# Seven instead of six of the eight contraction slices of the experts' gate and up products in upper and lower parts

## The reference, cut to what matters

```python
def moe(h, combine, w_gate, w_up, w_down):      # 16 experts, D_EXPERT = 256
    out = jnp.zeros_like(h)
    for e in range(N_EXPERTS):
        a = jax.nn.silu(h @ w_gate[e]) * (h @ w_up[e])
        out = out + combine[..., e:e + 1].astype(h.dtype) * (a @ w_down[e])
    return out
```

## Time and profile before

| | |
|---|---|
| median of three runs | 479.05 us (478.69 to 479.23) |
| the profiled execution | 479.01 us |
| its span in the trace | 477.3 us |
| TensorE busy | 431.7 us, 90% |
| VectorE busy | 313.1 us, 66% |
| ScalarE busy | 215.8 us, 45% |
| mean granted TensorE clock | 0.966 of full speed |

### The profile page before, as it was taken

The page is one execution under the profiler, slowest core; times in us unless marked ns, Lnnn a source line. Parts: engine busy times, 40 slices in busy tenths (PEclk is TensorE's granted clock), DMA queues, the critical chain, the costliest instruction groups (busy, mean ns, idle before and its releaser), DMA issues.

```text
span 477.3 us, 5118 instructions
## 1 busy us (share of the span) xinstructions
PE 431.7 (90%) x1824; PEld 280.4 (59%) x1824; DVE 313.1 (66%) x485; ACT 215.8 (45%) x360; POOL 107.4 (22%) x129
## 2 busy tenths in 40 slices
PE   5999999999999999999999999999999999998000
PEld 2444674477664544446687776777777777775000
DVE  3699969485403576776484166788778777783287
ACT  3121470151966810114211146788678777783151
POOL 7870000370065200000007410222332223211000
PEclk9999999999999999999999999999999999999655
DMA  8992007505993511110720249999999999611463
GB/s 271 381 359 81 0 2 109 126 22 153 409 420 137 214 56 44 44 44 12 297 90 0 36 145 426 408 421 419 406 373 368 377 396 356 247 52 43 150 251 149
DMA packets 37319, 98.95 MB, mean 207 GB/s; under 512 B 16976, under 2 KB 22688, under 8 KB 30624
## 3 DMA queue, kind: packets, MB, share of 16 engines
q1 hardware_dynamic: 28512, 88.45, 49.6%
q0 software_dynamic: 5088, 8.49, 5.0%
q10 hardware_dynamic: 3696, 1.71, 1.4%
HBM read 91.18 MB, written 14.17 MB: 221 GB/s over the span
## 4 chain that ended last, share of the span: by engine, by line
PE 73%; DVE 14%; DMA 5%; ACT 4%; issue 2%; SPq 1%; POOLq 0%; DVEq 0%; ACTq 0%
PE bank L1017 11%; PE bank L1189 9%; PE bank L858 6%; PE bank L1163 5%; PE bank L1168 4%; PE bank L1172 4%; PE bank L1176 4%; PE bank L1090 3%; PE bank L1092 3%; PE bank L1091 3%; DMA region_b<-in_ssm_par 3%; PE bank L1104 3%; PE bank L1147 3%; ACT region_a L632 2%; PE bank L874 2%
## 5 line engine op out<-in xcount | busy, mean ns | idle before, releaser
L1017 PE MATMUL bank<-region_b,region_e 128*128 128x512 f32 x128 | 58.3, 601 | 0.6 <-DVE region_f L1480 0.6
L858 PE MATMUL bank<-region_e,region_a 128*128 128x512 f32 x128 | 56.0, 595 | 0.0
L858 PEld LDWEIGHTS bank<-region_e,region_a 128*128 128x128 f32 x128 | 24.0, 190 | 29.7 <-issue 28.7
L1017 PEld LDWEIGHTS bank<-region_b,region_e 128*128 128x128 f32 x128 | 23.2, 190 | 25.0 <-issue 23.6
L1168 PE MATMUL bank<-gate_up_upper,tokens_upper 128*128 128x512 f32 x96 | 36.2, 459 | 0.0
L1172 PE MATMUL bank<-gate_up_upper,tokens_lower 128*128 128x512 f32 x96 | 29.8, 392 | 0.0
L1631 DVE TENSOR_TENSOR gate_up_lower<-region_a,gate_up_upper 128x1024 fp32r<-128x1024 f32 x24 | 28.0, 1221 | 2.4 <-ACT gate_up_upper L781 2.4
L517 POOL DMA_INDIRECT slot_scratch<-io_t,slot_i x8 | 8.5, 1058 | 93.4 <-issue 93.4
L530 POOL DMA_INDIRECT expert_scratch<-region_g,inv_t x8 | 11.4, 1429 | 78.4 <-ACT region_g L806 78.4
L865 PE MATMUL bank<-region_e,region_a 128*128 128x512 f32 x48 | 22.3, 627 | 5.0 <-DMA region_a<-in_w_in 5.0
L1090 PE MATMUL bank<-ple_gate_upper,hidden_upper 128*128 128x512 f32 x64 | 26.5, 415 | 0.0
(11 more groups left out here) (310 smaller groups left out, 936.4 us busy)
## 6 DMA issues: line engine op xcount, KB each, us to landing
region_a<-in_w_exp_gate SPq DMA_DIRECT2D x8, 1024.0 KB, 9.0
region_a<-in_w_exp_up SPq DMA_DIRECT2D x8, 1024.0 KB, 17.5
region_a<-in_w_exp_down SPq DMA_DIRECT2D x8, 1024.0 KB, 17.6
region_a<-in_w_in SPq DMA_DIRECT2D x3, 1536.0 KB, 17.8
region_b<-in_w_out SPq DMA_DIRECT2D x1, 4096.0 KB, 14.4
region_b<-in_w_exp_gate SPq DMA_DIRECT2D x4, 1024.0 KB, 9.5
region_b<-in_w_exp_up SPq DMA_DIRECT2D x4, 1024.0 KB, 17.5
region_b<-in_w_exp_down SPq DMA_DIRECT2D x4, 1024.0 KB, 17.3
```

Source lines behind the costliest of these rows:

```text
L858: last = mm(bank[bank_i][:], w[:, k, m * P:(m + 1) * P], xT[:, k, :], start=(k == 0), stop=(k == KD - 1))
L1017: last = mm(bank[WO_AT[half][group]][:], hdT[:, k, t * P:(t + 1) * P], w_o[:, k, half * 512:half * 512 + 512], start=(i == 0), stop=(i == ...
```

## The change

Seven slices go in parts, and one (slice 0) stays float32. The pieces in which the weights are rounded and subtracted are no longer three of two slices but four: `K_PARTS` has one slice first, and then three pieces of two. ScalarE's copy of the tokens is one slice in float32 and three and four slices rounded (before: two, two and four), VectorE's subtraction of the tokens three and four slices (before: two and four).

```diff
--- before.py
+++ after.py
@@ -41,7 +41,9 @@
 EPS = 1e-5
 NEG = -1.0e30
 BIG = 3.0e38
-KS = 6
+KS = 7
+K_PARTS = ((0, 1), (1, 3), (3, 5), (5, KS))
+NK = len(K_PARTS)
 CAP = P
 OVER = 7
 SLOT_TILES = NE + OVER
@@ -769,17 +771,17 @@
             def hgT_copy(e, r):
 
                 ac.wait_ge(S["pe_hgT"], e + 1)
-                a.activation(hgT[:, r, 0:2, :], bank[B_TOK[0]][:, 0:2 * P].rearrange("p (k s) -> p k s", k=2), ACT.Copy)
-                a.activation(x_hi[r][:, 0:2 * P], bank[B_TOK[0]][:, 2 * P:4 * P], ACT.Copy).then_inc(S["hgT_evac"], 1)
-                a.activation(x_hi[r][:, 2 * P:6 * P], bank[B_TOK[1]][:], ACT.Copy).then_inc(S["hgT_evac"], 1)
+                a.activation(hgT[:, r, 0, :], bank[B_TOK[0]][:, 0:P], ACT.Copy)
+                a.activation(x_hi[r][:, 0:3 * P], bank[B_TOK[0]][:, P:4 * P], ACT.Copy).then_inc(S["hgT_evac"], 1)
+                a.activation(x_hi[r][:, 3 * P:7 * P], bank[B_TOK[1]][:], ACT.Copy).then_inc(S["hgT_evac"], 1)
 
             def gate_up_upper(b, loads):
 
                 ac.wait_ge(S[f"e_in{b}"], 48 * loads)
-                for c in range(KS // 2):
-                    at = (KD - KS + 2 * c) * DE
-                    a.activation(gu_hi[:].rearrange("p (u n) -> p u n", u=2)[:, :, 2 * c * DE:2 * (c + 1) * DE],
-                                 ebuf[b][:, 0:4096].rearrange("p (u n) -> p u n", u=2)[:, :, at:at + 2 * DE], ACT.Copy).then_inc(S["gu_hi_set"], 1)
+                for lo, hi in K_PARTS:
+                    at = KD - KS
+                    a.activation(gu_hi[:].rearrange("p (u n) -> p u n", u=2)[:, :, lo * DE:hi * DE],
+                                 ebuf[b][:, 0:4096].rearrange("p (u n) -> p u n", u=2)[:, :, (at + lo) * DE:(at + hi) * DE], ACT.Copy).then_inc(S["gu_hi_set"], 1)
 
             def expert(e, b, loads, last=False):
                 r = b % 2
@@ -1161,18 +1163,18 @@
                 w_lo = gu_lo[b][:].rearrange("p (u k n) -> p k u n", u=2, k=KD)
                 for k in range(KD - KS):
                     mm(out_, hgT[:, r, k, :], w[:, k], start=(k == 0), stop=False)
-                C = KS // 2
-                for c in range(C):
+                C = NK
+                for c, ks in enumerate(K_PARTS):
                     pe.wait_ge(S["gu_hi_set"], C * e + c + 1)
-                    for k in (2 * c, 2 * c + 1):
+                    for k in range(*ks):
                         mm(out_, x_hi[r][:, k * P:(k + 1) * P], w_hi[:, k], start=False, stop=False)
                     if c == 0:
                         pe.wait_ge(S["gu_lo_set"], (C + 1) * e + 1)
-                    for k in (2 * c, 2 * c + 1):
+                    for k in range(*ks):
                         mm(out_, x_lo[:, k * P:(k + 1) * P], w_hi[:, k], start=False, stop=False)
-                for c in range(C):
+                for c, ks in enumerate(K_PARTS):
                     pe.wait_ge(S["gu_lo_set"], (C + 1) * e + c + 2)
-                    for k in (2 * c, 2 * c + 1):
+                    for k in range(*ks):
                         last = mm(out_, x_hi[r][:, k * P:(k + 1) * P], w_lo[:, KD - KS + k], start=False, stop=(k == KS - 1))
                 return last
 
@@ -1620,15 +1622,16 @@
 
                 dv.wait_ge(S["hgT_evac"], 2 * e + 2)
                 r = b % 2
-                tt(x_lo[:, 0:2 * P], bank[B_TOK[0]][:, 2 * P:4 * P], x_hi[r][:, 0:2 * P], ALU.subtract)
-                tt(x_lo[:, 2 * P:6 * P], bank[B_TOK[1]][:], x_hi[r][:, 2 * P:6 * P], ALU.subtract).then_inc(S["gu_lo_set"], 1)
+                tt(x_lo[:, 0:3 * P], bank[B_TOK[0]][:, P:4 * P], x_hi[r][:, 0:3 * P], ALU.subtract)
+                tt(x_lo[:, 3 * P:7 * P], bank[B_TOK[1]][:], x_hi[r][:, 3 * P:7 * P], ALU.subtract).then_inc(S["gu_lo_set"], 1)
                 w = ebuf[b][:, 0:4096].rearrange("p (u n) -> p u n", u=2)
                 w_lo = gu_lo[b][:].rearrange("p (u n) -> p u n", u=2)
                 w_hi = gu_hi[:].rearrange("p (u n) -> p u n", u=2)
-                for c in range(KS // 2):
-                    dv.wait_ge(S["gu_hi_set"], KS // 2 * e + c + 1)
-                    at = (KD - KS + 2 * c) * DE
-                    tt(w_lo[:, :, at:at + 2 * DE], w[:, :, at:at + 2 * DE], w_hi[:, :, 2 * c * DE:2 * (c + 1) * DE], ALU.subtract).then_inc(S["gu_lo_set"], 1)
+                for c, (lo, hi) in enumerate(K_PARTS):
+                    dv.wait_ge(S["gu_hi_set"], NK * e + c + 1)
+                    at = KD - KS
+                    tt(w_lo[:, :, (at + lo) * DE:(at + hi) * DE], w[:, :, (at + lo) * DE:(at + hi) * DE],
+                       w_hi[:, :, lo * DE:hi * DE], ALU.subtract).then_inc(S["gu_lo_set"], 1)
 
             def lower_parts(e, b):
```

## The result

The changed kernel takes 480.05 us (479.56 to 481.13, eight runs) where the kernel before takes 478.78 (478.43 to 479.27, eight runs). The ratio is 1.0025, its 95% interval 1.0015 to 1.0034: 0.7 to 1.6 us slower. The forecast was +0.8 us and 479.8 us.

What follows compares the result with a forecast made beforehand. Late landings of the down weights' loads were taken to stop TensorE's row; the longer chain behind them moved the last down products' start from 433.43 to 434.24, +0.81 us on 479.01, so 479.8 us, range 477.5 to 480.6.

Steps and rivals of the forecast that it cites:

- The bound: Experts' stage: landings of the down weights' loads, 10.0 us apart, stop TensorE's row of 9.71 us an expert.
- the window at 412 us: 412.0 to 417.1 us: DMA engines busy 0.47 on average, read as one or a few engines setting the landing.
- D(11): Start of the down matmuls behind expert 11's token transposes on TensorE; forecast within 0.1 us of before.
- A(13): ScalarE's start on expert 13's weights after waiting for their landing; 407.16 before, forecast within 0.3 us of it.
- The chain behind T: From an expert's token transposes through VectorE's subtractions to the next expert's down matmuls: 9.60 us before, 10.33 forecast.
- "0.56": VectorE: time between its last gate and up weights' piece and the down weights' subtraction, carried over unchanged in the sum.
- The chain behind A: From ScalarE's start on landed weights to the next expert's down matmuls: 7.49 us before, 8.00 forecast.
- hidden: ScalarE's fourth rounding piece, 0.51 us in a row, claimed to end before VectorE is ready for the down weights.
- A + 5.6: End of ScalarE's rounding of the down weights, counted in us from its start on the landed weights.
- The landings: Loads of the down weights: assumed to land unmoved; this case gave +0.81 us and had a chance of 0.55.
- load 13: Load of expert 13's down weights; every 0.1 us it lands late was priced as 0.1 us at the end.
- the fourth rival: Loads come later: requests slide with the down products, 0.3 to 0.9 us more, 480.4 with 0.6; chance 0.15.

Runs made afterwards that it cites:

- kernels without gathers: Kernel before and changed kernel, gathers of the tokens of experts 4 to 15 replaced by one 4 KB row each: 478.16 us (0.9983) and 476.54 us (0.9953).
- spread slots: Token slot s put on partition 2 (s mod 64) + s div 64: changed kernel 476.06 us (0.9943), kernel before 477.78 us (0.9969).
- products only: Kernel before with TensorE's part of the change alone, one float32 slice and seven in parts, suppliers as before: 479.16 us, ratio 1.0001.
- ScalarE cut: Parts only with ScalarE's small weights' piece cut from 2 x 256 to 2 x 16 columns, VectorE's left whole; run once for the trace, no time given.
- parts only: Changed kernel with its ScalarE and VectorE work kept, but TensorE doing two float32 slices and six in parts: 479.75 us, ratio 1.0019.
- its two cuts: Parts only with VectorE's, or else ScalarE's, small weights' piece cut from 2 x 256 to 2 x 16 columns; each run once for the trace, no time given.
- late wait: Changed kernel with the eight down matmuls needing only upper weights first, the wait for the lower part behind them: 479.81 us, ratio 1.0017.

## Why the prediction was right, and where it was not

**The number.** Forecast 479.8 us, measured 480.05; forecast +0.8 us, measured +1.27 by the medians. A part of the closeness is luck: the forecast was added to the profiled execution of before, 479.01 us, and the median of its eight runs is 478.78. The difference was 0.5 us short, mostly by the landings below.

**TensorE.** 0.17 us an expert was right: the full row is 9.53 us, forecast 9.55.

**The bound.** Right, and shown three times: TensorE's part alone gains nothing, the kernels without gathers gain 1.7 us, and so do those with spread slots. The reading of the window at 412 us, most DMA engines done and a few setting the landing, fits the runs with spread slots, though no view shows one engine. The Trainium skill (DMA: Bandwidth & Descriptors, "Why a DMA increments its semaphore by 16 and not by 1") says that the count is full only when the last engine has finished. That alone doesn't say that an earlier request lands no earlier, as the prediction had it; it takes a last engine that is never out of work as well. The runs bear the conclusion out where the slots are not spread: in products only D(11) is 0.46 us earlier than before and A(13) 0.10 later.

**The chain behind T.** Forecast 10.33 us, measured 7.69 + 2.29 + 0.14 = 10.12. The step that failed is "0.56" between VectorE's last piece and the down weights, which was carried over as if it were work. It was in part a wait for ScalarE (0.34 us is enough, as the rows with ScalarE cut show), whose rounding ends at 331.33 + 1.94 = 333.27 in the earlier trace rows and lets VectorE start at 333.30 in the earlier trace rows. The small piece came out as forecast: 4.09 us for four pieces against 3.50 for three, so 0.59 (forecast 0.60). Alone, behind a landing, it takes 0.69. The Trainium skill (VectorE: DVE Perf Modes, section on the TRN2 errata) has (N + 151) / 0.96 ns for it, 0.69 us, and the trace agrees. VectorE's four pieces in a row, and its rows at the landing of expert 13:

```profile
327.96 4.09 DVE L1633 TENSOR_TENSOR gate_up_lower<-region_b,gate_up_upper 128x512 fp32r<-128x512 f32 x4
...
407.24 0.69 DVE L1633 TENSOR_TENSOR gate_up_lower<-region_b,gate_up_upper 128x512 fp32r<-128x512 f32 x1 [0.53 <-ACT gate_up_upper L783]
...
411.60 0.42 DVE L1639 TENSOR_TENSOR act_lower<-bank,act_upper 128x256 fp32r<-128x256 f32 x1
412.16 2.29 DVE L1641 TENSOR_TENSOR down_lower<-region_a,down_upper 128x2048 fp32r<-128x2048 f32 x1
```

**The chain behind A.** Forecast 8.00 us, measured 414.60 - 406.58 = 8.02. The size was right and the reason was not: ScalarE was called hidden. Its rows at the same landing:

```profile
406.58 3.48 ACT L783 ACTIVATE gate_up_upper<-region_b 128x512 fp32r<-128x512 f32 x4 [1.05 <-DMA region_b<-in_w_exp_down]
409.96 0.36 ACT L798 ACTIVATE act_upper<-bank 128x256 fp32r<-128x256 f32 x1
410.22 1.91 ACT L800 ACTIVATE down_upper<-region_a 128x2048 fp32r<-128x2048 f32 x1
```

The rounding of the down weights ends at 412.13, and VectorE starts on them at 412.16, 0.2 us after its own row was through (411.60 and the 0.34 that the activations' lower part takes in the rows with ScalarE cut). The prediction had even computed ScalarE's end, A + 5.6, by its terms 5.55, and called it hidden behind VectorE's, which by its sum is A + 5.57 and has the inherited wait in it. Since both engines got one piece more, the sum was the same.

**The landings.** Assumed unmoved, and the sum gave +0.81. In the two traces A(13) is 0.7 and 1.3 us later. With 0.2 us off for the chain behind T and 0.7 on, the sum is +1.3 as in the first trace and the medians. So the step that failed here is the term that was put at nothing, the landings, by "D(11), behind which load 13 is asked for, stays within 0.1 us of before". This case was priced as the fourth rival, with 0.15. D(11) is 103.27 and 103.23 in the changed kernel and 102.85 and 102.89 before, 0.4 us later. The longer chain behind a landing explains it: in the first trace A(10) is 376.29 - 281.05 = 95.24, and 95.24 + 8.02 = 103.26. ScalarE's rows on expert 10's weights, and TensorE's row at D(11):

```profile
376.29 3.48 ACT L783 ACTIVATE gate_up_upper<-region_a 128x512 fp32r<-128x512 f32 x4 [0.91 <-DMA region_a<-in_w_exp_down]
...
384.32 0.47 PE L1191 MATMUL bank<-down_upper,act_upper 128*128 128x512 f32 x1 [0.47 <-DVE down_lower L1641]
```

What a later D(11) does is seen where TensorE's row is 9.71 us as before. In parts only and its two cuts D(11) is 103.35 to 103.40, and A(13) 125.10 to 125.41. From one to the other it is 21.75 to 22.01 us, as in the kernel before (21.96 and 21.79): the load slides with its request. So about 0.4 of the 0.7 and 1.3 us come from there. In the changed kernel the distance is 22.26 and 22.86 us, and this rest is open. TensorE being ahead is not the cause by itself (products only: D(11) 102.39, A(13) 124.91), though in the late wait, with D(11) at 102.49, A(13) is 126.51. What lies between may be the order in which weights, gathers and scatters meet on the most loaded DMA engines; no view shows one engine, and this was not tested.

## What to carry to other kernels

Before an engine's work is shortened, look for the next thing that is already late: here waits of 0.2 to 1.3 us of one supplier for landings, growing from expert to expert, told that the landings and not TensorE set the pace. A gap between two instructions on a supplier is not part of its work: ask which engine ended just before it, or an added cost is booked to the wrong one. When transfers are outstanding and the mean share of the DMA engines is a half, look whether the filled rows lie in one half of the partitions, and try to spread them first: here the other savings, 1.7 us on TensorE and 1.7 by the late wait, counted only after that.

## What the runs showed of the hardware

The place of the filled rows in the partitions decided here how fast loads land that have nothing to do with them. With the same bytes it was 367 GB/s with the rows in the lower half and 394 with the rows spread, and the landings were 10.0 us apart, or came in time for a row of 9.53. Asking for loads earlier did not make them land earlier while the rows lay in the lower half: D(11) 0.46 us earlier gave A(13) at 124.91 for 124.81, and in the late wait 0.7 to 0.8 us earlier than in the changed kernel gave 126.51 for 125.53 and 126.09, in one trace. And an element-wise instruction in a row of its like costs about 0.09 us less than alone: 0.59 and 0.69 us for VectorE's 512 columns.
